# The recurrent scan in 64x64 products alone, with the inverse and its transpose as one job and one ScalarE copy of 128x1024

## The reference

```
def step(S, inp):
    w_t, k_t, v_t, kk_t, kka_t = inp[:5]
    S = (S * w_t[:, :, None, :]
         - jnp.einsum('bhij,bhj->bhi', S, kk_t)[..., None] * kka_t[:, :, None, :]
         + v_t[..., None] * k_t[:, :, None, :])
    y = jnp.einsum('bhij,bhj->bhi', S, inp[5]) if emit else None
    return S, y
```

## Time and profile before

| | |
|---|---|
| median of 3 runs | 3102.48 us (3100.88 to 3104.81) |
| the profiled execution's own time, as its span | 3107.0 us |
| PE products, weight loads | 28892 and 28892, busy 91% and 79% of the span |
| DVE, ACT | busy 59% and 39% |
| the scan, from its first product to the next stage | 1226 to 1900 us |

### The profile page before, as it was taken

How to read it: one execution, slowest core, us unless ns; L and a number is a source line. 1 busy time by engine, 2 the same in 40 slices (tenths; PEclk the granted TensorE clock), 3 DMA queues, 4 the chain that set the end, 5 groups by cost and what they waited for, 6 DMA issues and landing times. The chain is left out here.

```text
span 3107.0 us, 66043 instructions
## 1 busy us (share of the span) xinstructions
PE 2828.0 (91%) x28892; PEld 2454.0 (79%) x28892; DVE 1827.1 (59%) x2841; ACT 1219.8 (39%) x2024; POOL 18.9 (1%) x25
## 2 busy tenths in 40 slices
PE   4988989999997998898899988899998898889998
PEld 4977989999996887677777776688886685678887
DVE  7656775655446644666666655755567644466642
ACT  4326343222224433555555543433334324454421
POOL 0011000000000000000000000000000000000000
PEclk9999989999996999999999998899998898999999
DMA  6320223333321323100000003355531210123332
GB/s 256 121 87 23 89 94 124 127 138 126 122 80 57 114 96 128 32 24 10 25 26 26 26 13 112 120 181 178 176 111 57 61 42 8 55 75 96 101 94 83
DMA packets 89981, 272.88 MB, mean 88 GB/s; under 512 B 9441, under 2 KB 14689, under 8 KB 89569
## 3 DMA queue, kind: packets, MB, share of 16 engines
q1 hardware_dynamic: 85088, 258.17, 24.4%
q10 hardware_dynamic: 4608, 10.49, 1.0%
HBM read 252.11 MB, written 16.52 MB: 86 GB/s over the span
## 5 line engine op out<-in xcount | busy, mean ns | idle before, releaser
L427 DVE TENSOR_TENSOR weights_low<-raw_weights,weights_high 128x1024 fp32r<-128x1024 f32 (+3 forms) x333 | 356.5, 1072 | 704.5 <-ACT weights_high L396 703.8
L396 ACT ACTIVATE weights_high<-raw_weights 128x1024 fp32r<-128x1024 f32 (+3 forms) x333 | 310.9, 935 | 975.1 <-PE psum L223 934.2
L223 PE MATMUL psum<-mlp_in_high,weights_high 128*128 128x512 f32 (+1 forms) x1120 | 371.4, 368 | 21.5 <-DVE mlp_in_low L964 16.4
L223 PE MATMUL psum<-mlp_in_low,weights_high 128*128 128x512 f32 (+1 forms) x1120 | 369.9, 367 | 0.0
L223 PE MATMUL psum<-mlp_in_high,weights_low 128*128 128x512 f32 (+1 forms) x1120 | 369.7, 367 | 0.0
L223 PEld LDWEIGHTS psum<-mlp_in_high,weights_high 128*128 128x128 f32 x1120 | 208.7, 190 | 49.3 <-issue 17.6
L223 PE MATMUL psum<-hidden_high,weights_high 128*128 128x384 f32 (+1 forms) x768 | 229.5, 352 | 0.0
L223 PE MATMUL psum<-hidden_low,weights_high 128*128 128x384 f32 (+1 forms) x768 | 229.5, 352 | 0.0
L223 PE MATMUL psum<-hidden_high,weights_low 128*128 128x384 f32 (+1 forms) x768 | 229.4, 352 | 0.0
L223 PEld LDWEIGHTS psum<-mlp_in_low,weights_high 128*128 128x128 f32 x1120 | 209.1, 190 | 24.2
L223 PEld LDWEIGHTS psum<-mlp_in_high,weights_low 128*128 128x128 f32 x1120 | 208.8, 190 | 24.3
(11 more groups left out here) (477 smaller groups left out, 5581.2 us busy)
## 6 DMA issues: line engine op xcount, KB each, us to landing
raw_weights<-in_mlp_w SPq DMA_DIRECT2D x96, 512.0 KB, 4.3
mod_space<-in_ada SPq DMA_DIRECT2D x56, 512.0 KB, 3.7
pool_u<-in_ada SPq DMA_DIRECT2D x56, 512.0 KB, 3.6
raw_weights<-in_w_up SPq DMA_DIRECT2D x44, 512.0 KB, 3.5
work<-in_ada SPq DMA_DIRECT2D x32, 512.0 KB, 4.8
raw_weights<-in_mlp_w SPq DMA_DIRECT2D x64, 256.0 KB, 2.9
raw_weights<-in_w_down SPq DMA_DIRECT2D x16, 512.0 KB, 3.5
raw_weights<-in_w_in SPq DMA_DIRECT2D x12, 512.0 KB, 4.8
```

Of the source, the lines that this page charges most:

```text
L223: last = nc.tensor.matmul(out[:, a, :] if wide else out, w[:, cols], x[:, at, t0:t1], start=first, stop=final)
L396: nc.scalar.activation(halves_of(ph, j)[0], raw_of(ph, j), ACT.Copy).then_inc(high.sem, 1)
L427: nc.vector.tensor_tensor(lo, raw_of(ph, j), hi.bitcast(F32), ALU.subtract).then_inc(split.sem, 1)
```

## The change

The scan's products are all of 64x64 now.

- **X** (L2492 and L2501 of the changed kernel) makes 32 products instead of 16: the new inverse into the lower halves of two banks and, by products with the operands exchanged, its transpose into the upper halves. ACT moves both by one copy of 128x1024 (L2714) to `XX`. **U** is left for the first level alone, as 16 products with the identity (L2463). T makes the transposed part alone.
- **E** and **K** write to rows chosen by another index than they read, so that all four quarters are used; the copies of E, and those of M, N, Z and others, keep their sizes, but E's two become one of 128x1024 (L2721).
- **tok** becomes 7 jobs of 24 products with the identity (L2590) and one copy of 128x768 (or two halves). `lora`, `bonus`, `sums`, `spread`, `ymean`, `yvar`, `yspread` are divided into 64x64 pieces too. Prep jobs use banks 4 and 5 together, each waiting for the keeper of the one before; `bonus` takes bank 7.
- **The ring** (`ring_slots`) has a third pair, banks 6 and 7, for Z, U, X, T and E, after the bonus and the sum of y have left them.
- The masks (`wkv_masks`) are laid out by level to fit.

```diff
@@ solve: products of U, Z, X and T on PE
-                        for n in range(4):
-                            c = slice(n * P, (n + 1) * P)
-                            last = nc.tensor.transpose(ps[:, 7, c], x[:, c], core.ident[:, :])
+                        for h in range(2):
+                            for j in range(2):
+                                for d in range(2):
+                                    for o in range(2):
+                                        f, to, c = rows_of(o), rows_of(d), (h * 2 + j) * CHUNK
+                                        last = nc.tensor.matmul(ps[to, b + o, c:c + CHUNK], X1[f, i, unit(h, d, j)], EYE[f, :],
+                                                                start=True, stop=True)
...
+                        if name == "X":
+                            for h in range(2):
+                                for same in range(2):
+                                    for side in range(2):
+                                        for o in range(2):
+                                            d, j = (same, side) if level % 2 else (side, same)
+                                            f, to, c = rows_of(side), rows_of(o), (h * 2 + same) * CHUNK
+                                            nc.tensor.matmul(ps[to, b + side, c:c + CHUNK], XX[f, g, 1, t_columns(level - 1, h, d, j, o)],
+                                                             Z[f, level, g % 2, z_columns(level, h, d, j, o)], start=True, stop=True)
+                        for h in range(2):
+                            for o in range(2):
+                                for d in range(2):
+                                    for j in range(2):
...
+                                        last = nc.tensor.matmul(ps[to, b + side, c:c + CHUNK],
+                                                                Z[f, level, g % 2, z_columns(level, h, d, j, o)],
+                                                                XX[f, g, 1, t_columns(level - 1, h, d, j, o)], start=True, stop=True)
@@ E on PE
-                                        f, u = rows_of(o), unit(h, d, j)
-                                        n = (d * 2 + j) * P
-                                        last = nc.tensor.matmul(ps[f, b + h, n:n + P], XT[f, i, u],
+                                        f, to, n = rows_of(j), rows_of(o), (h * 2 + d) * P
+                                        last = nc.tensor.matmul(ps[to, b + j, n:n + P], XX[f, i, 1, t_columns(len(LEVELS) - 1, h, d, j, o)],
@@ keepers on ACT
-                        last = act(by_tile(MX[:, i % GROUPS, 512:1024]), filled(b), ACT.Copy)
+                        last = act(XX[:, i % GROUPS, :, :].rearrange("p s (o c) -> p s o c", o=2),
+                                   ps[:, b:b + 2, :].rearrange("p o (s c) -> p s o c", s=2), ACT.Copy)
...
-                        for h in range(2):
-                            last = act(MX[:, i, h * 512:(h + 1) * 512], ps[:, b + h, :], ACT.Copy)
+                        last = act(two(MX[:, i, :]), ps[:, b:b + 2, :], ACT.Copy)
@@ tok on PE
-                        for j in range(3):
...
-                            last = nc.tensor.transpose(ps[:, prep_bank(k, TURN + n), j * P:(j + 1) * P],
-                                                       src[:, t * P:(t + 1) * P], core.ident[:, :])
+                        for p in range(tiles):
+
+                            t = tile_of((n - 1) % 2, p) if 1 <= n <= 4 else p
+                            for o in range(2):
+                                for h in range(2):
+                                    f, to = rows_of(h), rows_of(p % 2 if 1 <= n <= 2 else o)
+                                    c = (p // 2 * 2 + o if 1 <= n <= 2 else p) * CHUNK
+                                    last = nc.tensor.matmul(ps[to, 4 + h, c:c + CHUNK], src[f, at_chunk(t, o)], EYE[f, :],
+                                                            start=True, stop=True)
```

More of the change, by code:

```diff
@@ L2045, in solve_jobs @@
     for g in range(GROUPS):
-        jobs += [("M", g, 2, "SV" if g else "S"), ("N", g, 2, "V"), ("I", g, 2, "V")]
-    jobs += [("K", 0, 1, "S"), ("K", 1, 1, "S"), ("K", 2, 2, "S")]
-    for i in range(SOLVES + 2):
+        jobs += [("M", g, "SV" if g else "S"), ("N", g, "V"), ("I", g, "V")]
+    jobs += [("K", g, "S") for g in range(GROUPS)]
+    for i in range(SOLVES + 1):
         if i < SOLVES:
-            jobs.append(("Z", i, 2, "V"))
+            jobs.append(("Z", i, "V"))
         if i < GROUPS:
[L2052 to L2056, removed]
@@ L2057, in solve_jobs @@
-    jobs += [("E", g, 2, "S") for g in range(GROUPS)]
-    for g in range(GROUPS):
-        jobs += [("P", g, 2, "V"), ("B", g, 2, "V")]
-    return jobs + [("Y", 0, 2, "V")]
-def woven_stages():
[L2066 to L2073, removed]
+            jobs.append(("U", i, "S"))
@@ new lines, in solve_jobs, with ring_slots @@
+        if i >= 1:
+            jobs.append(("X" if i - 1 < SOLVES - GROUPS else "T", i - 1, "S"))
+    jobs += [("E", g, "S") for g in range(GROUPS)]
+    for g in range(GROUPS):
+        jobs += [("P", g, "V"), ("B", g, "V")]
+    return jobs + [("Y", 0, "V")]
+def ring_slots(jobs):
+    used = {0: -2, 2: -1, 6: [name for name, _, _ in jobs].index("Z")}
+    held, place, earlier = {}, {}, {}
+    for at, (name, i, _) in enumerate(jobs):
+        b = min((0, 2, 6) if name in "ZUXTE" else (0, 2), key=lambda b: used[b])
+        place[name, i], earlier[name, i] = b, (held.get(b), False)
+        held[b], used[b] = (name, i), at
+    for job, (before, _) in earlier.items():
+        if before is None:
+            earlier[job] = held[place[job]], True
+    return place, earlier
@@ new lines, in woven_stages @@
+def woven_stages():
+    at = {("M", 0): [("tok", 0), ("step", 1)], ("N", 0): [("tok", 1), ("step", 2)],
+          ("I", 0): [("tok", 2), ("step", 3)], ("M", 1): [("tok", 3), ("step", 4)],
+          ("N", 1): [("tok", 4), ("step", 5)], ("I", 1): [("tok", 5), ("step", 6)],
+          ("M", 2): [("tok", 6), ("step", 7)], ("N", 2): [("step", 8)],
+          ("I", 2): [("bonus", 0), ("step", 9)],
+          ("K", 0): [("lora", 0), ("step", 10)], ("K", 1): [("lora", 1), ("square", 0), ("decay", 0)],
+          ("K", 2): [("ystate", 0), ("lora", 2), ("decay", 1)],
+          ("Z", 0): [("ysum", 0), ("lora", 3)], ("Z", 1): [("keys", 0), ("power", 0)],
@@ L2144, in wkv @@
             kept_v[name, i] = n_v
[L2145 to L2150, removed]
+    job_index = {(name, i): n + 1 for n, (name, i, _) in enumerate(jobs)}
     n_jobs = len(jobs)
@@ L2566, in stage @@
                         if q:
[L2567 to L2571 removed]
+                            pe.wait_ge(*(lora_kept(q, 2 * n) if n else turn_kept(q - 1, 6)))
@@ L2572, in stage @@
+                        for h in range(2):
+                            for d in range(2):
+                                f, c = rows_of(d), which * P + h * HEAD
+                                last = nc.tensor.matmul(ps[rows_of(h), b + d, 0:T0 // 2], ups[f, c:c + HEAD],
+                                                        (lora_w, lora_a)[which][f, a * T0 // 2:(a + 1) * T0 // 2], start=True, stop=True)
+                        last.then_inc(prep_done.sem, 1)
                     elif name == "sums":
@@ L2727, in _ @@
                 for k in phases():
-                    for name, i, _, keeper in jobs:
+                    for name, i, keeper in jobs:
                         if 0 <= k < DT and "S" in keeper:
```

378 lines of the change are left out of this document (199 added, 179 removed).

## The result

The changed kernel took **3192.9 us** as the median of 4 runs (3189.5 to 3201.2), the kernel before on the same chip 3103.6 us (3100.9 to 3108.8): a ratio of 1.0287, 95% interval 1.0268 to 1.0306. Measured a second time, beside the experiments, it took 3199.2 us for 3101.9, ratio 1.0312 (1.0298 to 1.0326). So it is slower by 89 to 97 us; the forecast was 97.

The account below looks back on a forecast made before the run. PE's work bounds the kernel before, instruction packets the changed scan: a pass of 93 us for 80.4, over eight passes +101, lead-in and last readout -4, sum +97 on the 3102.48 us median, so 3200 us; range 3130 to 3285 us.

Parts of the forecast that it names:

- What bounds the kernel before: Recurrent scan: PE sets the time, busy 72.8 of 80.4 us a pass, with arrival of its instructions a near second bound.
- these gaps: Solve rounds: idle 0.17 us at each tile size change, 57 times a pass, 9.7 us, all removed by the change.
- PE's own work, -14.8 us a pass: Steady scan pass: no tile size changes and E, K and small products cheaper, less added tok and X products: -14.8 us.
- The packets: Scan: PE's program arrives 250 instructions at a time; a pass grows from 17.0 to 23.7 such packets, some 51 more altogether.
- The price: Scan: time per packet when PE is always behind, taken as 3.8 us, with 3.5 and 4.15 as limits.
- the two parts that I gave to the packets: Scan pass: M to I, 5.5 packets, 20.9 us, and the solve, 12.1 packets, 45.8 us.
- the two that I gave mostly to other waits: Scan pass: bonus to the second Z, about 12 us, and E to Y, 15 us with waits for DVE and ACT.
- The copy of 128x1024: Solve: ScalarE's single copy of X, at most 1.19 us, is covered by the two other groups' work.
- Rival A: Scan: PE's own work decides after all, a pass loses 14.8 us, 2980 us in total; chance 0.12.
- Rival B: Scan: packets come at 3.3 us, a pass stays within 1 us of 80.4, 3102 us, no change; chance 0.05.
- Rival C: Scan: PE's clock falls too, costing some 6 us a pass more in E, ystate, lora and bonus, 3250 us; chance 0.10.

Follow-up runs that it names:

- X wide: The kernel before with X alone in 8 products of 64 rows by 128x128, copied out by ScalarE and VectorE: 3148.3 us, ratio 1.0139.
- the first three runs: Changed kernel with Z on two quarters, 3204.6 us; each Z product streaming its columns twice, 3205.6 us; 16 one-column products added to every Z, 3319.3 us.
- idle products: 16 one-column products, read by nobody, added to every Z: 3319.3 us (1.0691) in the changed kernel, 3213.1 us (1.0344) in the kernel before.
- the tok jobs' 51 us: Changed kernel with five of seven tok jobs back as 128x128 transposes, expected 51 to 55 us faster by packets: 3179.6 us, ratio 1.0242.
- the wide products: The kernel before with products of 64 rows by 128x128 for Z, for Z and X, or for X alone: 3185.2, 3202.0 and 3148.3 us.

## Why the prediction was right

**What bounds the kernel before.** PE's own work, with packets close behind: borne out in part. For it: removed packets gave next to nothing, and X wide cost what its own work says. Against a single bound: added work showed to a third (Z on two quarters), and removed work not at all (K and E). The balance was closer than I wrote; "these gaps are the first thing that this change removes" promised a gain that the packets would have eaten already in part. How it divides is open.

**PE's own work, -14.8 us a pass.** The busy time went from 72.8 to 65.1 us a pass, -7.7. It also holds the stretched products at the lower clock (0.95 for 0.98 in five passes), and a busy second is not own work to the letter, so the term is not tested closely. Of its parts that can be read alone, E agrees (2.65 us for a forecast of 2.6), and so do the 0.17 us gaps but for the few behind lora.

**The packets.** 51 more, as forecast. The price was forecast at 3.8 us, and the restarts shown are 3.74, 3.85 and 3.75 us apart. But over the solve it comes to 3.6. By parts of the pass shown: M to I 20.9 forecast, 19.8 measured; bonus to the second Z 12, 13.75; the solve 45.8, 43.8; E to Y 15, 16.3. So the two parts that I gave to the packets were 3.0 us too long in the forecast, and the two that I gave mostly to other waits 3.1 us too short. By the means of five passes it is 2.8 too long (the solve) and 1.5 too short (bonus to the second Z). The mechanism was right; that the pass, forecast at 93 us, came out at 92.1 is in part luck, since the two errors cancel in part. The scan, from its first product to the readout's, was to be about 770 us for 674. It took 770 (1229.0 to 1999.1 us) for 676 (1227.1 to 1903.2).

**The copy of 128x1024.** Forecast as covered: right. Z waits 0.8 us for it in the scan.

**Rival A, own work decides.** It falls with the first three runs: some 34 and 42 us of added work showed as 5 or 6 and not at all in the solve, and 7680 instructions, whose products take 0.46 us a round at the full clock, 55 us in all, cost 120. The Trainium skill says in "Runtime: NRT & Kernel Launch", section "Instruction fetch mechanics", that the fetch is hidden because the sequencer is slower than the refill; this case's trace disagrees, with 137.6 us of stops in 590. The same section says that the next page of instructions is fetched while the current one runs; the rows agree, for the packet of 1497.5 comes while PE works on, from 1496.64 until it stops at about 1498.8.

**Rival B, 3.3 us a packet.** Nearer than I thought: the solve comes to 3.6 us a packet, and single restarts lie as little as 3.36 us apart (1655.81 and 1659.17). But no part of the pass comes down to 3.3.

**Rival C, the clock.** The granted clock did fall a little, 0.95 for 0.98 over five passes, 0.90 in the E to Y above. I had placed 6 us a pass on it; the pass came out at 92.1, so at most a few us of that are in it. With the idle products solves at clocks of 0.83 and 0.75 took 58.6 and 57.9 us: under packets the clock is covered. In the kernel before with its idle products it was not, 98 us for 89.

**What I had wrong** is, besides the price and the two parts, in the expectations: the price of Z on two quarters (0.28, not 0.5 us), the tok jobs' 51 us (a part's own floor), the new K and E in the kernel before (no gain for 10 to 26 us), and the wide products, where a copy chain and a larger round were missing.

## What to carry to other kernels

Count TensorE's instructions as a resource beside its time: where a stage has stops marked "issue" inside jobs, at equal counts and each behind a packet of the instruction queue, splitting products into smaller ones cost 3.6 to 3.9 us for each 250 instructions here, however little they compute. An fp32 product of this kernel counts four, a transpose two. But removing instructions pays only up to the waits that they cause, so sum those waits over the stage first, and price every copy behind a product before changing its shape.

## What the runs showed of the hardware

- While PE is behind, a packet shows in the DMA view about 1 us after a restart (1494.0 after 1493.05, 1497.5 after 1496.64, 1501.5 after 1500.38), and the next restart is 2.6 to 3.0 us after the packet. Read so, the distance is a sum of two parts; what sets either was not tried.
- A product of one column costs TensorE as much as one of 64 in such a series: 16 of them took 0.46 us from start to start, as the 16 of Z did.
- VectorE's predicated copy takes 0.73 us for 64 partitions by 512 as for 128 by 512, and ScalarE's 0.59 for both; two short copies are no substitute for a long one.
- Products that share an output half and alternate the rows took 0.84 us for 16, those that keep to two quarters on the diagonal 0.98 (K, half of its 1.95 us for 32), those that go round all four 0.56.
